# A two-block transformer layer on one core: the first block's attention heads taken in pairs

## The reference, cut to what matters

```python
s = einsum('bhqd,bhkd->bhqk', q, k) * scale       # causal, 256 queries in two blocks of 128
if fcum is not None:                              # fox only
    s = s + fcum_q - fcum_k
s = where(mask, s (+ relative bias), NEG_INF)
p = softmax(s)                                    # swa: with one more logit, the sink
o = einsum('bhqk,bhkd->bhqd', p, v)               # heads are 64 wide; mla queries and keys are 96 wide
```

## Time and profile before

| | |
|---|---|
| median of 3 runs | 3441.03 us (3437.82 to 3443.74) |
| the profiled execution | 3441.03 us, of which the span of the trace is 3438.8 us |
| TensorE busy over the span | 3108.5 us, 90% |
| VectorE, ScalarE, GpSimd busy | 56%, 37%, 10% |
| mean granted clock of TensorE | 0.98 |
| read from HBM | 898.81 MB |

### The profile page before, as it was taken

One profiled execution on the slowest core, in us unless ns is written; L12 is line 12 of the kernel. 1 busy time (PEld: TensorE's weight loads), 2 busy tenths in 40 slices (PEclk: granted clock), 3 DMA queues, 4 the chain that ended last, 5 costly groups with the idle time before them and its releaser, 6 DMA issues.

```text
span 3438.8 us, 43469 instructions
## 1 busy us (share of the span) xinstructions
PE 3108.5 (90%) x18098; PEld 2422.4 (70%) x18098; DVE 1923.2 (56%) x2855; ACT 1278.3 (37%) x2353; POOL 353.5 (10%) x358
## 2 busy tenths in 40 slices
PE   8998999999999999999989999999897768777776
PEld 8887887999999999997979989444452223322222
DVE  6545455555555555666665543555556565555554
ACT  4434444444444445555444343222222222222221
POOL 1000000000000000200001001222232222221120
PEclk9999899999999999999999999999999999999999
DMA  7434444555555555544445445999999999999998
GB/s 221 143 123 164 143 136 142 201 184 184 184 184 182 182 183 182 192 167 151 156 160 187 156 138 194 430 431 431 430 421 431 430 427 430 431 431 431 431 431 344
DMA packets 99282, 911.06 MB, mean 265 GB/s; under 512 B 10313, under 2 KB 20937, under 8 KB 23949
## 3 DMA queue, kind: packets, MB, share of 16 engines
q0 software_dynamic: 36864, 536.89, 36.5%
q1 hardware_dynamic: 48816, 344.95, 29.1%
q10 hardware_dynamic: 13404, 26.45, 2.5%
HBM read 898.81 MB, written 9.44 MB: 264 GB/s over the span
## 4 chain that ended last, share of the span: by engine, by line
PE 67%; DMA 21%; DVE 6%; ACT 4%; issue 1%; ACTq 0%; DVEq 0%; POOL 0%; POOLq 0%
PE sums L551 15%; PE sums L553 15%; PE sums L552 15%; PE sums L963 10%; DMA area<-in_uv,cst 9%; DMA hT<-in_uv,cst 5%; DMA ringx<-in_uv,cst 3%; DMA ring<-in_uv,cst 3%; PE sums L919 2%; PE sums L575 2%; PE sums L577 1%; PE sums L576 1%; DVE area L2050 1%; ACT area L1008 1%; ACT cst L1008 1%
## 5 line engine op out<-in xcount | busy, mean ns | idle before, releaser
L1558 DVE TENSOR_TENSOR wl<-ring,wh 128x1024 fp32r<-128x1024 f32 x612 | 748.9, 1229 | 673.8 <-ACT wh L1008 672.9
L1008 ACT ACTIVATE wh<-ring 128x1024 fp32r<-128x1024 f32 x612 | 642.7, 1054 | 511.9 <-PE sums L553 441.5
L1008 ACT ACTIVATE cst<-cst 128x1 f32<-128x1 f32 (+2 forms) x786 | 234.2, 299 | 902.4 <-DVE cst L2050 839.9
L963 PE MATMUL sums<-area,cst 128*128 128x512 f32 x984 | 455.6, 608 | 100.8 <-ACT cst L1008 100.7
L963 PEld LDWEIGHTS sums<-area,cst 128*128 128x128 f32 x984 | 182.4, 192 | 355.9 <-issue 189.6
L2050 DVE CUSTOM_DVE_ANT_0 area<-area 128x2048 f32<-128x2048 f32 x123 | 281.8, 2292 | 257.3 <-DMA area<-in_uv,cst 257.3
L963 PE MATMUL sums<-ringx,cst 128*128 128x512 f32 x656 | 304.1, 609 | 63.5 <-ACT cst L1008 63.5
L551 PE MATMUL sums<-inputs,wh 128*128 128x256 f32 x1152 | 334.1, 290 | 19.8 <-DVE wl L1558 12.3
L552 PE MATMUL sums<-inputs,wh 128*128 128x256 f32 x1152 | 327.6, 284 | 0.0
L553 PE MATMUL sums<-inputs,wl 128*128 128x256 f32 x1152 | 327.4, 284 | 0.0
L551 PE MATMUL sums<-normed,wh 128*128 128x256 f32 x1024 | 290.0, 283 | 0.0
(11 more groups left out here) (322 smaller groups left out, 5886.3 us busy)
## 6 DMA issues: line engine op xcount, KB each, us to landing
ring<-in_w_in_a SPq DMA_DIRECT2D x66, 1024.0 KB, 4.8
ring<-in_w_up SPq DMA_DIRECT2D x64, 1024.0 KB, 4.8
ring<-in_w_down SPq DMA_DIRECT2D x64, 1024.0 KB, 4.8
ring<-in_w_out SPq DMA_DIRECT2D x32, 1024.0 KB, 4.9
ring<-in_w_in_b SPq DMA_DIRECT2D x16, 1024.0 KB, 4.9
ring<-in_w_xk SPq DMA_DIRECT2D x16, 1024.0 KB, 5.1
ring<-in_w_xv SPq DMA_DIRECT2D x16, 1024.0 KB, 5.0
ring<-in_w_xq SPq DMA_DIRECT2D x16, 1024.0 KB, 4.8
```

The costliest lines, as they stand in the source:

```text
L963: mm = te.matmul(sums[t][:, 512 * i:512 * i + 512], diag[:, n % 2, :], v[:, 512 * i:512 * i + 512], start=False, stop=n % 128 == 127)
L1008: return sc.activation(out, in_, f, **kw)
L1558: ve.tensor_tensor(wl[:, j % 3, :], ring[:, load % 3, j % 2 * 1024:j % 2 * 1024 + 1024], wh[:, j % 3, :], ALU.subtract).then_inc(lo_in, 1)
```

## The change

`S` gets a fourth buffer. The heads are handled as pairs on all engines, and nothing is computed otherwise than before. `scores(p)` makes the scores of both heads of a pair, block by block, first head, second head. `values(p)` makes the values of both in the same way. The two transposes of a pair stay separate. One iteration has four `yield`s for a pair, as two iterations had before, and each of the three calls has two `yield`s more in all (22 for eight heads instead of 20, 54 for 24 instead of 52).

```diff
-                for x in range(n + 2):
-                    if x + 1 < n:
-                        scores(x + 1)
-                    if 0 <= x - 2 < n:
-                        values(x - 2)
-                    yield
-                    if 0 <= x - 1 < n:
-                        turn(x - 1)
-                    yield
+                for p in range(n + 2):
+                    if 0 <= p - 2:
+                        values(p - 2)
+                    yield
+                    if 0 <= p - 1 < n:
+                        turn(2 * p - 2)
+                    yield
+                    if p <= n:
+                        if 0 <= p - 1:
+                            turn(2 * p - 1)
+                        yield
+                        if p + 1 < n:
+                            scores(p + 1)
+                        yield
```

In it `n` is now the number of pairs. The new bodies of `scores` and `values` on TensorE:

```diff
+                def scores(p):
+                    u = u0 + 2 * p
+                    on.wait_ge(biased, u)
                     for qt, a, b in BLOCKS:
+                        for e in range(2):
+                            hd, bank = heads[2 * p + e], banks[3 + e]
+                            f = "f" in hd
+                            mm = te.matmul(bank[:, a:b], hd["q"][:, qt * P:(qt + 1) * P], hd["k"][:, 0:b - a],
+                                           start=True, stop=not f)
...
+                def values(p):
+                    u = u0 + 2 * p
+                    bank = banks[6 + u // 2 % 2]
+                    on.wait_ge(out_off, u // 2 - 1)
+                    on.wait_ge(pt_in, u + 2)
+                    for part, y, x in ((0, slice(0, 256), slice(0, 256)), (1, slice(128, 256), slice(256, 384))):
+                        for e in range(2):
+                            hd, r = heads[2 * p + e], slice(64 * e, 64 * e + 64)
+                            mm = te.matmul(bank[r, y], hd["v0"][:, part, hd["v"]:hd["v"] + 64], PT[e][:, x],
+                                           start=part == 0, stop=part == 1)
```

VectorE's and ScalarE's orders follow. `divide` is the scaling, `biased_max` the bias and maxima, `exps` the exponentials, `turned_back` the copy to `PT`:

```diff
 VectorE
+                for p in range(n + 2):
+                    if 0 <= p - 1 < n:
+                        divide(2 * p - 2)
+                    if p < n:
+                        biased_max(2 * p)
+                    yield
+                    if 0 <= p - 1 < n:
+                        divide(2 * p - 1)
+                    if p < n:
+                        biased_max(2 * p + 1)
+                    if 0 <= p - 2:
+                        outputs(p - 2)
+                    yield
+                    if p <= n:
+                        yield
+                        yield
 ScalarE
+                for p in range(n + 2):
+                    if p < n:
+                        exps(2 * p)
+                    yield
+                    if 0 <= p - 1 < n:
+                        turned_back(2 * p - 2)
+                    if p < n:
+                        exps(2 * p + 1)
+                    yield
+                    if p <= n:
+                        if 0 <= p - 1:
+                            turned_back(2 * p - 1)
+                        yield
+                        yield
```

More of the change, by code:

```diff
@@ L263, in program @@
         bias = ar(16, 384)
-        S = [ar(384) for _ in range(3)]
+        S = [ar(384) for _ in range(4)]
         PT = [ar(384) for _ in range(2)]
@@ L639, in turn @@
                     for j in range(3):
-                        mm = te.transpose(banks[5][:, j * P:(j + 1) * P], S[u % 3][:, j * P:(j + 1) * P], ident)
+                        mm = te.transpose(banks[5][:, j * P:(j + 1) * P], S[u % 4][:, j * P:(j + 1) * P], ident)
                     mm.then_inc(turned, 1)
[L643 to L653, removed]
@@ L655, in attention @@
-                scores(0)
-                for x in range(n + 2):
-                    if x + 1 < n:
-                        scores(x + 1)
-                    if 0 <= x - 2 < n:
-                        values(x - 2)
+                def values(p):
[8 more added lines that the diff above has]
+                                           start=part == 0, stop=part == 1)
+                            if part:
+                                mm.then_inc(valued, 1)
@@ L1127, in attention @@
             def attention(heads, u0):
-                n = len(heads)
-                for x in range(n + 2):
-                    yield
[L1131 to L1145, removed]
-                    yield
+                n = len(heads) // 2
@@ new lines, in exps @@
+                def exps(x):
+                    hd, u = heads[x], u0 + x
+                    Sx, nm, total = S[u % 4], stat[u % 4][:, 0:2], stat[u % 4][:, 2:4]
+                    on.wait_ge(maxed, u + 1)
+                    if "sink" in hd:
+                        act(stat[u % 4][:, 4:6], nm, ACT.Exp, bias=hd["sink"])
+                    for qt, a, b in BLOCKS:
+                        e = act(Sx[:, a:b], Sx[:, a:b], ACT.Exp, bias=nm[:, qt:qt + 1],
+                                accum_out=total[:, qt:qt + 1])
+                    e.then_inc(exped, 1)
@@ L1631, in attention @@
             def attention(heads, u0):
[L1632 to L1641, removed]
-                        on.wait_ge(v_seq, seq.n)
[L1643 to L1672, removed]
-                    yield
@@ new lines, in attention, with divide @@
+                n = len(heads) // 2
+                def divide(x):
+                    hd, u = heads[x], u0 + x
+                    Sx, total = S[u % 4], stat[u % 4][:, 2:4]
+                    on.wait_ge(exped, u + 1)
+                    if "sink" in hd:
+                        ve.tensor_tensor(total, total, stat[u % 4][:, 4:6], ALU.add).then_inc(v_seq, seq.one())
+                        on.wait_ge(v_seq, seq.n)
+                    ve.reciprocal(total, total).then_inc(v_seq, seq.one())
+                    on.wait_ge(v_seq, seq.n)
+                    if "gate" in hd:
+                        ve.tensor_tensor(total, total, gts[:, :, hd["gate"]], ALU.mult).then_inc(v_seq, seq.one())
+                        on.wait_ge(v_seq, seq.n)
+                    for qt, a, b in BLOCKS:
+                        d = ve.tensor_scalar(Sx[:, a:b], Sx[:, a:b], total[:, qt:qt + 1], None, ALU.mult)
+                    d.then_inc(divided, 1)
@@ new lines, in biased_max @@
+                def biased_max(x):
+                    hd, u = heads[x], u0 + x
+                    Sx, nm = S[u % 4], stat[u % 4][:, 0:2]
+                    on.wait_ge(turned, u - 3)
+                    on.wait_ge(scored, u + 1)
+                    ve.tensor_tensor(Sx, banks[3 + u % 2][:, 0:384], hd["bias"], ALU.add).then_inc(biased, 1)
+                    on.wait_ge(biased, u + 1)
+                    ve.tensor_reduce(nm[:, 0:1], Sx[:, 0:128], AX.X, ALU.max, negate=True)
+                    m = ve.tensor_reduce(nm[:, 1:2], Sx[:, 128:384], AX.X, ALU.max, negate=True)
+                    if "sink" in hd:
+                        m.then_inc(v_seq, seq.one())
+                        on.wait_ge(v_seq, seq.n)
+                        m = ve.tensor_scalar(nm, nm, hd["nsink"], None, ALU.min)
+                    m.then_inc(maxed, 1)
@@ new lines, in outputs @@
+                def outputs(q):
+                    hd, p = heads[2 * q + 1], u0 // 2 + q
+                    on.wait_ge(valued, 2 * p + 2)
+                    if hd.get("add"):
+                        on.wait_ge(out_off, p)
+                        ve.tensor_tensor(hd["out"], banks[6 + p % 2][:, 0:256], hd["out"], ALU.add).then_inc(out_off, 1)
+                    else:
+                        ve.tensor_copy(hd["out"], banks[6 + p % 2][:, 0:256]).then_inc(out_off, 1)
+                for p in range(n + 2):
[3 more added lines that the diff above has]
+                        biased_max(2 * p)
+                    yield
+                    if 0 <= p - 1 < n:
[4 more added lines that the diff above has]
+                        outputs(p - 2)
```

27 lines of the change are left out of this document (13 added, 14 removed).

## The result

| | median (lowest to highest), us | runs |
|---|---|---|
| before | 3440.51 (3437.82 to 3444.0) | 20 |
| changed | 3446.11 (3439.6 to 3456.53) | 20 |

The ratio is 1.0015, with a 95% interval of 1.0009 to 1.0022: no difference by the 0.2% bound, and slower by 5.6 us if anything. The forecast was 3428.5 us, range 3412 to 3440. In the profiled executions the span went from 3438.8 to 3447.4 us. TensorE, VectorE and ScalarE have as many instructions as before (18098, 2855 and 2353); TensorE's busy time fell by 13.8 us, from 3108.5, though more of it ran at the lower clock. So the products did become cheaper, and TensorE now waits.

A forecast was written before the change was run, and what follows sets the result against it. The prediction took the attention to be bounded by the cost of its products on TensorE. From 3441.0 us it took 25.0 for cheaper products (19.2 + 4.1 + 1.7) and added 12.5 of waits: 3428.5 us, range 3412 to 3440.

The forecast's parts named there:

- The products: TensorE's scores and values of paired heads get cheaper: 19.2 us gained in late heads, 4.1 in `mla`.
- Rival 2: Values of a pair don't overlap on TensorE, as both use all rows: 12.8 us of gain gone, 3441 us; chance 0.11.
- the choice of 0.98 over 1.62: TensorE time in us for a pair's values: 0.98 if the two heads overlap, 1.62 if not; 0.98 was taken.
- The `fox` term: Pairing the eight `fox` heads gains 3.5 us on products, less 1.8 for the clock: 1.7 us, between -2 and +5.
- The waits: TensorE waits for VectorE's scaling: 9.5 us in late pairs, 3 in `mla` and `fox`, together 12.5 in some 20 places.
- The clock outside `fox`: Loss to the 1.2 GHz clock was reckoned only among the `fox` heads; elsewhere the sum has no term for it.
- Costs of nothing: Two more yields per call move norms and compression behind `fox` some six pieces later, at no cost.
- Rival 3: The gain is swallowed in TensorE's idle behind `fox`, at norms, compression and output projection: 3435 to 3441 us; chance 0.09.
- Rival 4: Slower: every pair's second transposes meet the long chain, 20 x 2.8 = 56 us less 25: 3472 us; chance 0.07.
- the long chain: Ahead of a second head's transposes: another head's scaling, bias and maxima, `exps`, `spill_out`, `upper`, `lower`, scaling; 2.8 us wait.
- Rival 1: The waits are hidden as VectorE and ScalarE keep ahead; the whole 25.0 us arrives: 3416 us; chance 0.17.
- The forecast's own condition for being wrong: TensorE's waits for the scaling under 5 or over 20 us, or its idle behind `fox` growing by the gain.

The follow-up runs named there:

- e3: Changed kernel with the old yields, VectorE's second head two yields after the first, ScalarE one yield behind VectorE, second transposes a yield later: 3432.71 us, ratio 0.9978.
- e4: As e3, but the eight `fox` heads handled one by one as before the change: 3426.28 us, ratio 0.9960.
- e1: Kernel before, heads one by one, with only two more yields behind each of the three attention calls on all three engines: 3446.82 us, ratio 1.0015.
- e2: Changed kernel with its two extra yields per call taken out again: 3442.4 us, ratio 1.0006 against the kernel before.
- e6: As e3, but in each block of `fox` scores the 64-row products of both heads first, then the 8-row products of both: 3418.2 us, ratio 0.9934.
- e5: As e4, but within a pair all products of the first head ahead of all of the second, in scores and values: 3426.8 us, ratio 0.9957.

## Why the prediction was wrong, point by point

**The products: right.** Scores 1.04 for 1.06, values 1.00 for 0.98, `mla` score pairs 1.31 for 1.33. The `mla` stretch is 2.2 us shorter for a gain of 4.1 on products (4.0 by its own terms), with one wait of 1.6 us for the scaling. Rival 2 falls, and the rule on row groups that the forecast weighed (the Trainium skill, "TensorE: Matmul & The Clock Gate", section "The mechanism") is not borne out here: the pair's values use the same 128 rows and lose nothing. The products of the earlier trace rows had been the right neighbour, though with 15 rows they didn't show it for 128, so the choice of 0.98 over 1.62 was a guess that held.

**The `fox` term: wrong in sign.** The forecast took 3.5 us from the products, 1.8 off for the clock. The pairs cost 6.4 us (e3 to e4). The count of stretches at 1.2 GHz was right and their length lay at the upper end. With 27 us instead of 17 the clock takes 5 us and not 1.8, so that 3.5 - 5 = -1.5. Of the other 5 us the traces of e3 and e4 show 1.1 us more idle among the `fox` heads and 1.8 more at the norms behind them. The last 2 us are not settled: e4 also takes VectorE and ScalarE back to the single order there, and the clock varies from run to run by about 3 us.

**The waits: the chain right, the term too small.** The longest wait was forecast to a tenth. All the waits for the scaling are 12.6 us over the whole kernel, for 12.5 forecast, but in eight places and not in some 20, so that the sums agree partly by luck. What failed is that this was taken for the whole. The late heads have 17.9 us of waits where 9.5 stood in the sum. The 8.4 us are chiefly the wait for the bank, 6.5. The forecast listed `spill_out` as a link that delays others (0.8 us) and never asked who waits for `spill_out` itself.

**The clock outside `fox`: put at nothing.** The sum took a wait at its length and asked for the clock among the `fox` heads alone. Among the late heads the change brought 10.2 us at 1.2 GHz where there had been none, up to 5.1 us lost. The forecast had these heads 9.7 us faster (19.2 less 9.5), and they are 2.2 slower: 11.9 us off, by the 8.4 of waits and by the clock.

**"Costs of nothing": the step that failed outright.** "These pieces are work that TensorE must do anyway" is true of the pieces, and overlooks what they stood in front of. Behind `fox` 9.6 us went: 3.2 us by idle time (3.20 us at the norms for 0.54 and 2.0 at the second compression, less what other waits shrank), and the rest with the lower clock (1.00 to 0.87 over the norms, 0.77 to 0.67 ahead of the late heads, 0.89 to 0.82 over the whole). Over the whole kernel the yields cost 5.8 us by the medians of e1 and 3.7 by e2.

**The sum.** 3441.0 - 25.0 + 12.5 was forecast. By the runs, from medians: e6 shows what this pairing can give, -22.9. Then `fox` heads that don't overlap (+14.5: 3432.71 against 3418.2), bunching (+9.7), yields (+3.7). The sum is +5.0, and +5.6 was measured. It had to come out so, as each step is the distance between two of the kernels; it orders the losses and proves none.

**Rivals.** Rival 3 (3435 to 3441) had one of the two right places, behind `fox`, and was too mild by 5 us. Its counter-argument, that the chains behind `fox` shift with TensorE's progress, fails because the order shifted as well. Rival 4 (3472) is out: the long chain doesn't come with every pair. Rival 1 is out. The forecast's own condition for being wrong, waits outside 5 to 20 us, was drawn around the wait for the scaling and didn't fire. The range ended at 3440, since no rival had two costs in one and the slower rival was left out of it.

## What to carry to other kernels

In streams woven by hand, an edit that moves the count of yields by even two is an edit of all that comes behind: look there at what each engine has queued ahead of the next chain's first instruction, the emptying of banks and function tables among them. When the products of two items are put together on the bounding engine, leave the work of the helping engines spread out; here that was worth 9.7 us, as much as half of the 19.2 gained on the late heads' products. Ask of each helper's instruction not only whom it delays, but who waits for it. And look at the granted clock in every stretch that gets new waits, not only where it was low before.

## What the runs showed of the hardware

Values of two heads, 128 rows and 64 columns each, in different column halves, cost 1.00 us a pair against 0.98 for one head, even when all four passes of the first are queued ahead of the second's (1.01 in e5). The granted clock fell to 1.2 GHz while TensorE was busy without a gap, within or right behind the scores with 8-row products: windows of 8.3, 6.8, 10.2 and 3.4 us at the four `fox` pairs had a mean of 0.60, 0.52, 0.51 and 0.53. That the 8 rows are the cause was argued from where the stretches lie, not tried alone. And the same program has a different clock there from one execution to the next, 0.90 and 0.86, at a cost of 3 us.
